# Two-layer transformer kernel in f32: the down-projections take four and five pairs of input chunks as seven products, after three and three

## The reference, cut to what matters

```python
z = rmsnorm(h, norm_ffn_g)
ff = (silu(z @ w_ffn_gate) * (z @ w_ffn_up)) @ w_ffn_down        # 2048 -> 5632 -> 2048
h = h + ff
...
x = x + square(relu(hm @ w_up)) @ w_down                         # 2048 -> 8192 -> 2048
```

## Time and profile before

| | |
|---|---|
| runs of the kernel | 2528.99, 2530.42, 2530.89 us; median 2530.42 |
| profiled execution, first to last instruction (span) | 2528.4 us |
| the same execution's own time | not listed apart; all runs lie 0.6 to 2.5 us above the span |
| TensorE busy | 2509.3 us, 99%, 11904 instructions |
| VectorE busy | 1796.1 us, 71% |
| ScalarE busy | 1316.6 us, 52% |
| GpSimd busy | 409.8 us, 16% |
| DMA | 478.31 MB, mean 189 GB/s |

### The profile page before, as it was taken

One profiled execution on the slowest core, in us unless ns is written; L12 is line 12 of the kernel. 1 busy time (PEld: TensorE's weight loads), 2 busy tenths in 40 slices (PEclk: granted clock), 3 DMA queues, 4 the chain that ended last, 5 costly groups with the idle time before them and its releaser, 6 DMA issues.

```text
span 2528.4 us, 32741 instructions
## 1 busy us (share of the span) xinstructions
PE 2509.3 (99%) x11904; PEld 2111.7 (84%) x11904; DVE 1796.1 (71%) x2081; ACT 1316.6 (52%) x1769; POOL 409.8 (16%) x287
## 2 busy tenths in 40 slices
PE   9999999999999999999999999999999999999998
PEld 7889888888888888888889988888888888888887
DVE  5556554555788988899656766565669788978874
ACT  5445454444555544555545554455556545654653
POOL 1001100112212211212002301031132211221110
PEclk9999999999999999999999999999999999999999
DMA  7645556575656556655656655465565565556564
GB/s 244 202 146 152 170 169 191 191 237 180 199 192 203 194 193 208 196 201 195 231 176 186 182 149 158 146 218 174 160 194 194 194 203 183 198 194 214 177 220 155
DMA packets 251124, 478.31 MB, mean 189 GB/s; under 512 B 15152, under 2 KB 38368, under 8 KB 249840
## 3 DMA queue, kind: packets, MB, share of 16 engines
q1 hardware_dynamic: 248416, 464.20, 57.5%
q0 software_dynamic: 2256, 12.13, 1.4%
q10 hardware_dynamic: 320, 0.20, 0.0%
HBM read 474.36 MB, written 2.12 MB: 188 GB/s over the span
## 4 chain that ended last, share of the span: by engine, by line
PE 94%; DVE 2%; issue 1%; ACT 1%; POOL 0%; DMA 0%; ACTq 0%; POOLq 0%; DVEq 0%
PE acc L1536 75%; PE acc L1562 6%; PE unit L1562 4%; PE unit L1590 3%; PE psO L1562 2%; PE psS L1562 2%; PE psO L1761 1%; ACT w_hi L1268 1%; PE psS L1656 0%; DVE w_lo L1883 0%; DVE x_sb L2080 0%; PE unit L1656 0%; ACT p L1410 0%; DVE stat L2117 0%; PE psS L1727 0%
## 5 line engine op out<-in xcount | busy, mean ns | idle before, releaser
L1883 DVE TENSOR_TENSOR w_lo<-w_raw,w_hi 128x1024 fp32r<-128x1024 f32 (+6 forms) x592 | 716.6, 1221 | 480.0 <-ACT w_hi L1268 474.8
L1268 ACT ACTIVATE w_hi<-w_raw 128x1024 fp32r<-128x1024 f32 (+6 forms) x592 | 596.1, 1017 | 462.0 <-PE acc L1536 439.4
L1536 PE MATMUL acc<-w_hi,xT_hi 128*128 128x512 f32 (+4 forms) x2020 | 783.4, 388 | 3.7 <-DVE xT_lo L1991 1.8
L1536 PE MATMUL acc<-w_lo,xT_hi 128*128 128x512 f32 (+4 forms) x2020 | 772.0, 382 | 0.0
L1536 PE MATMUL acc<-w_hi,xT_lo 128*128 128x512 f32 (+4 forms) x2020 | 771.5, 382 | 0.0
L1536 PEld LDWEIGHTS acc<-w_hi,xT_hi 128*128 128x128 f32 x2020 | 379.4, 188 | 73.7 <-issue 5.5
L1536 PEld LDWEIGHTS acc<-w_lo,xT_hi 128*128 128x128 f32 x2020 | 379.1, 188 | 70.0
L1536 PEld LDWEIGHTS acc<-w_hi,xT_lo 128*128 128x128 f32 x2020 | 379.6, 188 | 66.1 <-issue 0.5
L1914 DVE TENSOR_TENSOR w_lo<-w_raw,w_hi 128x1024 fp32r<-128x1024 f32 (+1 forms) x204 | 281.3, 1414 | 51.2 <-ACT w_hi L1292 49.2
L1536 PE MATMUL acc<-w_hi,hT_hi 128*128 128x512 f32 x720 | 281.2, 391 | 0.0
L1536 PE MATMUL acc<-w_lo,hT_hi 128*128 128x512 f32 x720 | 280.2, 389 | 0.0
(11 more groups left out here) (441 smaller groups left out, 3128.7 us busy)
## 6 DMA issues: line engine op xcount, KB each, us to landing
w_raw<-in_w_in SPq DMA_DIRECT2D x168, 512.0 KB, 3.6
w_raw<-in_w_down SPq DMA_DIRECT2D x104, 512.0 KB, 4.3
w_raw<-in_w_up SPq DMA_DIRECT2D x100, 512.0 KB, 4.1
w_raw<-in_w_ffn_down SPq DMA_DIRECT2D x76, 512.0 KB, 4.5
w_raw<-in_w_ffn_gate SPq DMA_DIRECT2D x68, 512.0 KB, 4.3
w_raw<-in_w_ffn_up SPq DMA_DIRECT2D x68, 512.0 KB, 3.9
w_raw<-in_w_out SPq DMA_DIRECT2D x64, 512.0 KB, 4.0
s_raw<-in_w_up SPq DMA_DIRECT2D x28, 512.0 KB, 6.0
```

Source lines behind the costliest of these rows:

```text
L1268: act.activation(w_hi[:, slot, 0:kc, 0:n], w_raw[:, slot, 0:kc, 0:n], ACT.Copy).then_inc(hi_split, 1)
L1536: ins = pe.matmul(ac[t][:, 0:n], a[:, l0 + c, t * P:(t + 1) * P], w[:, slot, c, 0:n], start=start and c == 0 and m == 0, stop=stop and c = ...
L1883: dve.tensor_tensor(w_lo[:, slot, 0:kc, 0:n], w_raw[:, slot, 0:kc, 0:n], w_hi[:, slot, 0:kc, 0:n].bitcast(F32), ALU.subtract).then_inc(lo_ ...
```

## The change

- Each half (pair of blocks) of a down stage takes more pairs of chunks as sevens: four of twelve in the first half, five in the second, in all three stages. The plans are new.
- The sum `b_sum[0:2]` of these sevens is made by VectorE (`sums="dve"`), at the start of step `half` 0. The loops of the up-projections keep GpSimd's.
- The second and fourth seven of a half (`ring=(1, 3)`) have their raw weights in the ring, the others in `s_raw`.
- The input sums `h_sum` are made for five chunk pairs, in two portions: three before the first seven as before, two more by a step that stands before the second seven's `half` 0, with the split before the third's.
- ScalarE's high part of a weight sum now also waits for the input sums' low parts (`a_lo_split`), since they share places.
- The sums of xT give up part of their place: they are stored to DRAM (`keep_sums`) at `x_split`, and come back after each down stage (`sums_back`), both on GpSimd's queue. The first seven of the next loop waits for them.
- `shared` is done through a buffer of two rows: ScalarE copies psS, VectorE forms the common sums once and adds them to `x_sb`: 2, 2, 3 and 1 adds in four parts, where `shared_read` (banks free) comes in the third. Of the first half the last two parts stand behind the second and third tile of the second half; of the second half they stand after the last evacuation.
- The constants are loaded in three smaller pieces instead of one, and some tensors have other places.

The core of the diff:

```diff
-DOWN_PLANS = ("00101101S0101S1010S01", "00101S0101S1010S11001")
+DOWN = sevens((4, 5), ("00101101S01S01S01S01", "0010S10S10S10S11S01"), ring=((1, 3), (1, 3)), sums="dve")
+SUMMED = 3
...
+    def with_sums(steps, group, units):
+        n = group["summed"]
+        halves = [i for i, s in enumerate(steps) if s[0] == "half" and s[1] == 0]
+        i = halves[0]
...
+        j, k = halves[1], halves[SUMMED - 1]
+        return ([("h_sums", group, units, 0, SUMMED)] + steps[:i] + [("h_split", group, 0, SUMMED)] + steps[i:j] +
+                [("h_sums", group, units, SUMMED, n)] + steps[j:k] + [("h_split", group, SUMMED, n)] + steps[k:])
...
+        one, rest = block_pair(w, k0, 24, 0, needs, turn, DOWN["plans"][0], g[0], [both(x) for x in last])
+        two, left_over = block_pair(w, k0, 24, 1024, (), turn, DOWN["plans"][1], g[1], [[x] for x in rest])
+        return with_sums(one, g[0], units) + two + left_over + [("sums_back",)] * more
...
@@ gpsimd
+                elif s[0] == "x_split":
+                    pool.wait_ge(a_lo_split, at["sums"] + 1)
+                    for i, v in enumerate((a_sum_hi, a_sum_lo)):
+                        pool.dma_start(keep_sums[i], v[:].bitcast(F32).rearrange("p j i q -> p (j i q)")).then_inc(sums_kept, 16)
                 elif s[0] == "h_sums":
-                    units_read(pool, at["unit"] - 1 - 4)
-                    pool.wait_ge(seven_done, at["seven"] + 1)
-                    input_sums(hT, s[1], h_whole, h_sum)
+                    _, group, units, a, b = s
+                    units_read(pool, at["unit"] - 1 - units if a == 0 else at["unit"] - 1)
+                    pool.wait_ge(seven_done, at["seven"] + 1 - (a > 0))
+                    if a:
+                        pool.wait_ge(tile_done, at["tile"] - RING)
+                        pool.wait_ge(shared_added, at["added"])
+                    elif group["home"] == NEAR:
+                        pool.wait_ge(sums_kept, 32 * at["kept"])
...
+                elif s[0] == "sums_back":
+                    pool.wait_ge(seven_done, at["seven"] + 1)
+                    for i, v in enumerate((a_sum_hi, a_sum_lo)):
+                        pool.dma_start(v[:].bitcast(F32).rearrange("p j i q -> p (j i q)"), keep_sums[i]).then_inc(sums_back, 16)
@@ scalar
                     if h == 0:
                         act.wait_ge(seven_done, m + 1)
+                        act.wait_ge(a_lo_split, at["sums"])
...
+                elif s[0] == "shared" and s[2] == 0:
+                    act.wait_ge(seven_done, at["seven"] + 1)
...
+                    act.activation(to[:, 0], psS[:].rearrange("p i k -> p (i k)"), ACT.Copy).then_inc(p1_copied, 1)
@@ tensor
+                                if first and q == 0 and at["back"]:
+                                    pe.wait_ge(sums_back, 32 * at["back"])
@@ vector
                     if h == 0:
-                        B = s_raw[:].rearrange("p b c n -> p (b c) n")
+                        B = group_weights(s, at)
+                        if s[3]["sums"] == "dve":
+                            dve.wait_ge(x_summed, at["sums"])
+                            dve.wait_ge(b_lo_split, 2 * m + 2)
+                            dve.tensor_tensor(sum_[:, 0:2], B[:, 2:4], B[:, 0:4:2], ALU.subtract).then_inc(b_summed, 1)
                         dve.wait_ge(b_summed, 2 * m + 1)
...
                     if part == 0:
-                        dve.wait_ge(seven_done, at["seven"] + 1)
+                        dve.wait_ge(p1_copied, at["group"])
+                        dve.tensor_tensor(x_(0, 0), x_(0, 0), to[:, 0], ALU.add)
+                        after(dve.tensor_tensor(to[:, 1], to[:, 0], p7, ALU.add))
+                    elif part == 1:
+                        dve.tensor_tensor(to[:, 0], to[:, 1], p6, ALU.add)
+                        after(dve.tensor_tensor(to[:, 1], to[:, 1], p5, ALU.add))
                     else:
...
+                        if part == 2:
+                            dve.tensor_tensor(x_(0, 1), x_(0, 1), to[:, 0], ALU.add)
+                            dve.tensor_tensor(to[:, 0], to[:, 0], p5, ALU.add).then_inc(shared_read, 1)
+                            after(dve.tensor_tensor(x_(1, 0), x_(1, 0), to[:, 1], ALU.add))
+                            dve.wait_ge(shared_read, at["group"] + 1)
+                        else:
+                            dve.tensor_tensor(x_(1, 1), x_(1, 1), to[:, 0], ALU.add).then_inc(shared_added, 1)
```

More of the change, by code:

```diff
@@ L247, in block_steps, with block_pair @@
     return [("tile", b, k) for k in range(tiles_in(b))] + [("evac", b, (0, 1))]
[L250 to L256, removed]
+def block_pair(w, k0, kc, c0, needs, turn, plan, group, between=()):
+    b = [make_block(w, k0, kc, c0 + 512 * j, 512, "hT", 0, "add", c0 + 512 * j, needs, turn) for j in range(2)]
+    plain = [k for k in range(kc // CK) if not 1 <= k <= group["n"]]
+    k, q, out, part, between = [0, 0], 0, [], 0, [()] + list(between)
     for x in plan:
         if x == "S":
-            out.insert(-1, ("half", 0, q))
-            out.insert(-1, ("half", 1, q))
-            out.append(("seven", b[0], b[1], q))
+            i = max(n for n, y in enumerate(out) if y[0] == "tile")
+            out[i:i] = [("half", h, q, group) for h in range(2)]
+            out.append(("seven", b[0], b[1], q, group))
             q += 1
@@ L266, in block_pair @@
         k[j] += 1
-        out += turns.pop(0) if turns else ()
-        if q == SEVENS and part < 4:
-            out.append(("shared", c0, part))
+        out += between.pop(0) if between else ()
+        if q == group["n"] and part < 4:
+            out.append(("shared", c0, part, group))
             part += 1
@@ L272, in block_pair @@
             out.append(("evac", b[j], (0, 1)))
[L273 to L280, removed]
+    assert k == [len(plain)] * 2 and q == group["n"], (plan, k, q)
+    return out, [("shared", c0, p, group) for p in range(part, 4)]
 def both(name):
@@ L480, in number @@
 def number(steps):
-    out, shapes, wrote, seen, apart, sevenths = [], {}, {}, {}, set(), {}
-    c = dict(tile=0, lead=0, block=0, unit=0, split=0, hidden=0, seven=0, places=0, pairs=0, relus=0, silus=0, sums=0, squares=0, root=0, gained=0)
+    out, shapes, wrote, seen, apart, sevenths, held = [], {}, {}, {}, set(), {}, {}
+    c = dict(tile=0, lead=0, block=0, unit=0, split=0, hidden=0, seven=0, places=0, group=0, added=0, kept=0, back=0, after=2, relus=0, silus=0, sums=0, squares=0, root=0, gained=0)
     ahead = 0
@@ L506, in number @@
             shapes[at["tile"]] = (min(CK, b["kc"] - CK * k), b["n"])
+            at["summed"] = held.get(at["tile"] - RING)
         elif kind == "lead":
@@ L517, in number @@
             c["seven"] += 1
-            c["places"] += 1
+            c["places"] += own
+            if q == group["n"] - 1:
+                c["group"] += 1
+                c["after"] = 0
+        elif kind == "half":
+            at["seven_tile"] = c["tile"] + 1
+        elif kind == "h_sums":
+            at["added"] = c["added"]
+            if s[1]["home"] != NEAR and s[3] == 0:
+                s[1]["clear"] = c["tile"]
+        elif kind == "shared":
+            at["added"] = c["added"]
+            c["added"] += s[2] == 3
+            if s[2] == 3:
+                for j in range(2):
+                    wrote["shared", s[1] // 512 + j] = c["added"]
+        elif kind == "sums_back":
+            c["back"] += 1
         elif kind == "x_sums":
@@ L560, in number @@
                 c["split"] += TRANSPOSES[s[1]][6] in ("split", "gain", "halves")
+            at["shared"] = c["group"] if c["after"] < 2 else None
+            c["after"] += 1
             c["unit"] += 1
```

239 lines of the change are left out of this document (154 added, 85 removed).

## The result

| | before | after |
|---|---|---|
| median of the runs | 2530.47 us (2528.99 to 2530.89, 4 runs) | **2543.11 us** (2541.89 to 2547.07, 4 runs) |
| span of the profiled execution | 2528.4 us | 2540.2 us |
| mean granted clock | 0.999 | 0.997 |

The ratio is 1.0054, with a 95% interval of 1.0039 to 1.0068. The change makes the kernel slower, by 12.6 us where 6.7 were forecast. The measured time lies 1.1 us above the top of the range.

The account below looks back on a forecast made before the run. TensorE, busy 99% of the span, was taken as the bound. Terms -6.1 - 1.4 + 14.2 = +6.7 us on the 2528.4 us span gave 2535.1, plus 2.0 to the median: 2537.1 us, range 2524.5 to 2542.

Parts of the forecast that it names:

- The clock: Down-stage stops: half clock for 10 matmuls each would cost 6 us; counted only in a rival, not in the sum.
- rival D: Parked sums' transfers starve and delay the loops' first seven, or the clock falls: 6 us more, 2543 us; chance 0.08.
- The loops behind the stages: Loop entries after down stages: VectorE's backlog meets the first seven's due times; taken at nothing, bound 0 to 0.5 us each.
- Matmuls removed: Down stages: three more sevens in each of three stages remove 27 matmuls at 0.227 us, -6.1 us.
- The end of a stage: Stage end into the loop: earlier evacuation and buffered shared sums remove TensorE's waits for x_sb adds, -1.4 us.
- The chain before the first seven: Down stages: VectorE's added 1024-wide sum delays the low halves, 0.8 to 0.9 us a stage, 2.6 in all.
- The second portion: Before the first seven: GpSimd's later input sums alternate with VectorE; with the chain 4.7 us a stage, +14.2 us.
- Seam between sevens: Between a stage's two groups of sevens: b_sum_lo about on time, taken as 0, up to 0.3 us a stage.
- parking hidden: Sums of xT returning from DRAM after each stage's last seven fit within five tiles, 13.6 us, so cost nothing.
- constants free: Smaller constant loads and trig's new place cost nothing; constants arrive many tiles before bias_row needs them.
- The starving of GpSimd's transfers: Parked sums' return: transfers lack descriptors while VectorE holds the port, so the loops' first seven waits 2 us.
- Rival B: GpSimd's later input sums miss the critical moments: 2525.5 us, or 2522.9 with the 1.2 us chain hidden; chance 0.24.

Follow-up runs that it names:

- experiment 2: Kernel after with 14 useless matmuls filling TensorE's wait before the fourth product of each down stage's first seven; 2540.23 us.
- experiment 6: Kernel after without GpSimd's seventh-tile wait before the second portion, and with VectorE's new weight sum made a tile earlier; 2527.43 us.
- experiment 8: experiment 6 with four and four sevens, two plain tiles behind the last seven of a stage; 2527.71 us.
- experiment 7: experiment 6 with four and four sevens, five plain tiles behind the last seven of a stage; 2523.59 us.
- experiment 1: Kernel after with GpSimd's second portion of input sums held until both low halves of the first seven's weight sums are made; 2540.39 us.
- experiment 4: experiment 1 with VectorE's new 1024-wide weight sum of the first seven made a tile earlier; 2536.43 us.
- experiment 5: Kernel after without GpSimd's wait for the seventh tile, so the second portion of input sums follows the first at once; 2529.14 us.
- experiment 3: Kernel after with three and three sevens, the plans of before and no second portion, other new code kept; 2530.25 us.

## Why the prediction was right and wrong

- **The clock.** This is the step that failed. The prediction had the size ("if it fell to half for 10 matmuls at each stop, at 0.2 us more each, that is 6 us too") and put it into rival D, which had 0.08, as if it were another case than the forecast. It is not: the clock hangs on the stop that the forecast itself expected, since the earlier trace rows showed 1.46 us to be harmless and nothing about 3.7. So the sum held the clock at nothing without a reason. The runs showed 26 slow matmuls behind the three stops, 5.2 us. Filling the stop keeps the clock full and takes 4.2 us of lateness away (experiment 2); that kernel's 2540.2 us lie inside the range. As a bound from 0 to 6 us on top of the forecast, the clock would have brought the time into the range.
- **The loops behind the stages.** The second step that failed. The prediction wrote "I take nothing; 0 to 0.5 us each is the bound", and the loops took +2.6 us in the kernel after, +4.4 in experiment 6. The account looked only at the first due times of the loop, and the larger stops stand 95 and 138 us behind the entry (experiment 8).
- **Matmuls removed, -6.1.** Right: 11877 instructions. In experiment 7, with 18 fewer, the stages fall by 4.1 and before's stops, to the tenth.
- **The end of a stage, -1.4.** Right at the entry: the waits of the earlier trace rows are gone. From start to start they were worth 1.9.
- **The chain before the first seven, 0.8 to 0.9 a stage.** Right: 0.36 + 0.42 in experiment 1 (1.0 with the two matmuls behind the waits), and gone there with the sum a tile earlier (experiment 4).
- **The second portion, stop of 3.7 + 1.0.** The mechanism was right, the Trainium skill's exclusive lock (SBUF — State Buffer, "SBUF: two separate sides") agrees, and so does the order by turns of the earlier trace rows. The size was a little high: 3.37 us at psO and 0.2 to 0.9 behind it, 11.5 us in all for 14.2. Counted from the stage's first matmul, TensorE was ready for the first low part at 24.8 us as forecast, and the part was there at 28.2 in place of 28.4, since each of the turns took a little less than forecast. The wait for the second half was small in two stages because matmuls at the half clock stood before it (0.33 and 0.23); in the second stage the clock fell later, and it was 0.87. The stated high end of 6.0 a stage for "GpSimd's six operations whole, beside the 0.8" is 6.4 by the row prices, which changes nothing. Experiment 5 removes the collision without removing any work, and the stages fall by 14.3 us.
- **Seam between sevens, 0; parking hidden; constants free.** Right: the seam shows 0.06 us a stage, and experiment 3, which has the other two, lies at the time of before. The parked sums land 9.5 to 11.2 us after the first of the two copies is issued, and no wait of TensorE ends at them. The starving of GpSimd's transfers that the other half of rival D named was not seen. The Trainium skill (SBUF — State Buffer, "The "DVE blocks DMA" trap (SWDGE)") ties it to VectorE operations in a 2-port mode, a condition that the rival left out.
- **Rival B** ("no collision", 2525.5, or 2522.9 with the chain hidden) is the kernel of experiments 5 and 6, not the one given: 2529.1 and 2527.4, higher than B mainly by the loops' loss.

The sum by what was measured: -6.1 - 1.9 + 10.1 + 7.7 in the stages, + 2.6 in the loops, - 0.7 in the rest, is +11.7 on a span that grew by 11.8. That the time lies only 1.1 us above the range is in part luck: the stop was priced 2.7 us too high, which hid as much of the clock and the loops.

## What to carry to other kernels

Where two engines hold each other up in SBUF, place the one with slack by the other's critical chain, not by when its operands could at latest be there: here one wait that held GpSimd back, harmless for buffers, cost 14 us, and without it the same work cost the stages nothing. When a forecast contains a new stop of TensorE longer than any in the trace, price the clock behind it in the same case: here the two came together at all three stops of 3.2 us. And a saving made in a stage can be paid for behind its end: leave plain tiles behind the last piece of dense work, and compare the length of what follows, not only the waits at the seam.

## What the runs showed of the hardware

The granted clock against the length of TensorE's stop (in the view, no matmul in flight), after work at full clock:

| stop | kernels | stops behind which the clock fell to half | time at half |
|---|---|---|---|
| 1.4 to 1.5 us | the stop of the earlier trace rows, in each of the twelve traces | 0 of 12 | 0 |
| 1.8 and 2.0 us | experiments 4 and 1 | 1 of 3 each | 3.4 us each |
| 3.2 us | after | 3 of 3 | 3.4, 3.4, 6.8 us |
| the same stop filled with matmuls | experiment 2 | 0 of 3 | 0 |

What decides it at 2 us stayed open: equal stops in the three stages of one execution went either way. The other thing is that a stretch of the same code, with no wait at its entry, was 4.4 us longer for how the work ahead of it ended (experiments 7 and 8), with VectorE 10.5 us longer at about as many instructions, and its stretched instructions stood beside GpSimd's sums each time.
